# A two-layer hybrid decoder trunk on one core: the ring of expert weight buffers, the order of the shared product and the gather, and the first and last transfers

## The chip, the core and the metric

One core of one Trainium2 chip runs the whole program in one launch. The metric is the device time of that launch in microseconds (us), as the median of several runs; lower is better. TensorE is called PE below, VectorE DVE, ScalarE ACT, GpSimd POOL, and SyncE, which only issues transfers here, SP.

## What is computed

The reference runs two layers over 256 tokens of width 1024, all in float32. Each layer has three parts, each of them closed by a LayerNorm of alpha times its input plus its result:

```
mix = parallel_mixer(x, ...)            # short convolution branch and latent attention branch, gated
xat = memory_cross_attention(x, mem)    # k = mem @ w_xk, v = mem @ w_xv, 4 heads
ffn = moe_ffn(x, ...)                   # 64 experts of width 256, 8 per token, plus one shared expert

def experts(args):                      # every expert, weighted by its gate (zero where not chosen)
    hid = silu(einsum('btd,edf->btef', xt, w_gate)) * einsum('btd,edf->btef', xt, w_up)
    return einsum('btef,efd->btd', hid * gt[..., None], w_down)
shared = (silu(x @ ws_gate) * (x @ ws_up)) @ ws_down
```

The three weights of one expert are 1 MiB each, so the 64 experts of a layer are 192 MiB that must be read from HBM, and each is read once.

## The kernel before

Every engine has its own program, written out by hand, and they are ordered by semaphores. SP issues nearly all loads, in one fixed order; before a load into a buffer that was used earlier it waits (helper `alone`) until PE has read what lies there.

**Dense part of a layer.** 24 named loads (`LOADS`) of about 2 MiB go round six slots of the tile `ring`. PE multiplies them (`by_token`, `by_feature`, all through `accumulate`, L728) into the four PSUM banks `work0` to `work3`, which ACT and DVE copy out. The very first one is `xk0`, half of w_xk, which is multiplied with memT, the transposed memory; `mem` is loaded first of all, transposed by PE (L761) and copied by DVE (L1414).

**Routing.** DVE computes from the router scores which 8 experts each token takes, by a long chain of small instructions (L1701 to L1734), and signals `chosen_ready`. PE then computes the places of the tokens in each expert's list ("place", L1013, L1014). The shared expert's down product is eight matmuls into the PSUM banks `moe_sum0` to `moe_sum3` (`add_shared`, L1021), four behind "place" and four between the gathers. After the last one PE signals `shared_down`, which frees ring slot 5 (the load "down_router"). A gather (L1035) is four matmuls that select rows of x into a bank, which ACT (even chunks, L1361) or DVE (odd chunks, L1790) copies to SBUF; the first eight gathers of a layer alternate between banks 3 and 1.

**Experts.** They are taken in 32 pairs, eight pairs to a body, four bodies to a round (`expert_body`, L1099). There would be further rounds only if some expert had over 32 tokens of either half; in these runs there is one. A pair q of a body needs three units of 2 MiB: unit 3q and 3q+1 hold the gate and up weights, 3q+2 the two down weights. For a pair that is "not in halves" unit 3q is one expert and 3q+1 the other, and PE needs both to begin. For a pair "in halves" unit 3q holds the first half of the contraction for both experts and 3q+1 the second, so PE can begin with the first unit alone (`in_halves`). The order on PE in a pair is: gate and up (16 matmuls, L1128), half of the scatter of the pair before (L1082), a gather for a later batch (L1035), the transpose of the hidden rows (L1146), the other half of the scatter, the down product (8 matmuls, L1159), another gather. Below, units are numbered through a layer: unit m of body j is number 24j + m, and pairs are numbered 0 to 31.

**Buffers for the units.** Units 0 to 5 are the slots of `ring`; two more (6 and 7, tile `arena`) lie in memory that is free in the expert part; and one, `EXTRA`, lies in the first 4096 columns of `arena`. EXTRA is used once in a layer, for unit 8. `place_of` gives unit m of the first body its buffer, `wait_unit_read` gives the read that SP waits for before it loads:

```
if first:
    prev = m - UNITS - 1 if m <= 2 * UNITS else m - UNITS
elif second and m < UNITS:
    prev = m - (UNITS - 1) if m < UNITS - 1 else m - 2 * UNITS + 1
else:
    prev = m - UNITS
```

So a load waits for the read of the unit nine before it up to number 16, eight before it from 17 to 23, seven before it from 24 to 30 (31 finds its buffer free early), and eight before it from 32 on. The first nine units, numbers 0 to 8, are loaded in the dense part as their buffers come free; number 5 is the last of them to be issued, since it waits for `shared_down`. Number 9 waits for the read of number 0.

**The end.** After the second layer DVE normalises: token tile 0 is written by one instruction (L1506) and stored by SP (L599), tile 1 by two multiplies (L1511) and one add of 1024 columns (L1513), then stored whole (L601).

## Time and profile before

| | us |
|---|---|
| median of 3 runs | 1678.62 (1678.43 to 1679.38) |
| the profiled execution, its own time | 1679.52 |
| its span, first to last instruction | 1677.7 |
| PE busy in the span | 1618.2 (96%) |
| ACT busy, DVE busy, POOL busy | 280.5, 423.4, 80.5 |
| HBM read over the span | 507.64 MB, 303 GB/s mean |

The expert parts run from 380.7 to 838 us (first layer) and from 1204.8 to 1662 us (second layer); before each lies its dense part. PE is busy nearly everywhere, so what can be gained lies in the little idle time, and in what ended each stretch of it. A row of the profile's windows gives, for a stretch, each engine's busy time with its instruction count, the granted clock, the busy share of the 16 DMA engines and what they moved. A row of the waits names who waited for whom, total, number and longest. A row of the timeline has start, duration, engine, line, what it does, and in brackets the idle time before it with what ended it. [...]

### The profile page before, as it was taken

Reading aid. Unit: us, or ns where it says so; the run is one execution under the profiler, and the core shown is the slowest. Engines: PE = TensorE matmul, PEld = TensorE weight load, DVE = VectorE, ACT = ScalarE, POOL = GpSimd, SP = SyncE. Lnnn points to the kernel's source line nnn. Section 1 sums busy time; section 2 is a strip of 40 time slices with the busy share of each in tenths; the row PEclk is TensorE's granted clock in tenths of the full one; section 3 lists DMA queues with packets and bytes.
Section 4 is the critical chain, followed back from the end, with each engine's and each line's share of the span. In section 5 each row is a group of like instructions: output and inputs, shape, how many; then the busy total and the mean of one; then the engine's idle time right before and its main releaser. Section 6 shows DMA issues by size and latency. Waiting matters only on the chain.

```text
span 1677.7 us, 19829 instructions
## 1 busy us (share of the span) xinstructions
PE 1618.2 (96%) x8037; PEld 901.8 (54%) x8037; DVE 423.4 (25%) x886; ACT 280.5 (17%) x555; POOL 80.5 (5%) x92
## 2 busy tenths in 40 slices
PE   7999999999999999989999999999999999999996
PEld 5878867573333333333378786765633333333332
DVE  2122221162222222222222402112522222222223
ACT  1022011031111111111110410111311111111111
POOL 1000020030000000000030000201200000000000
PEclk9999999999999999999999999999999999999998
DMA  9246443469999999999980743434799999999995
GB/s 347 75 149 252 143 156 135 176 226 373 372 407 421 418 421 421 418 421 421 410 301 0 289 162 126 165 142 176 276 385 394 421 421 419 421 421 419 421 421 216
DMA packets 111240, 509.95 MB, mean 304 GB/s; under 512 B 8354, under 2 KB 12580, under 8 KB 68660
## 3 DMA queue, kind: packets, MB, share of 16 engines
q1 hardware_dynamic: 110592, 508.59, 76.2%
q8 instruction: 65, 1.06, 0.3%
q0 software_dynamic: 224, 0.12, 0.0%
q14 instruction: 19, 0.16, 0.0%
q10 hardware_dynamic: 340, 0.02, 0.0%
HBM read 507.64 MB, written 1.05 MB: 303 GB/s over the span
## 4 chain that ended last, share of the span: by engine, by line
PE 79%; DMA 12%; SPq 5%; DVE 3%; issue 1%; ACT 1%; DVEq 0%
PE work L728 38%; PE work L1128 20%; DMA ring<-in_w_up 11%; PE work L1159 9%; SPq L548 5%; PE moe_sum L1082 3%; PE work L1035 3%; PE moe_sum L1021 1%; DMA ring<-in_w_xk 1%; PE work L1146 1%; PE moe_sum L1074 1%; PE work L1042 0%; PE work L777 0%; PE work L864 0%; DVE arena L1721 0%
## 5 line engine op out<-in xcount | busy, mean ns | idle before, releaser
L1128 PE MATMUL work<-ring,arena 128*64 128x512 f32 x1536 | 365.5, 599 | 19.6 <-DMA ring<-in_w_up 12.4
L728 PE MATMUL work<-XT,ring 128*128 128x256 f32 (+1 forms) x1408 | 280.3, 360 | 1.3 <-DVE arena L1630 1.3
L728 PEld LDWEIGHTS work<-XT,ring 128*128 128x128 f32 x1408 | 247.5, 190 | 32.7 <-issue 3.0
L1128 PEld LDWEIGHTS work<-ring,arena 128*64 128x64 f32 x1536 | 118.4, 137 | 206.8 <-issue 194.7
L1159 PE MATMUL work<-ring,hidden 128*64 128x512 f32 x768 | 175.4, 598 | 1.0 <-DVE hidden L1829 1.0
L1836 DVE TENSOR_TENSOR out_lo<-work,out_hi 128x512 fp32r<-128x512 f32 x128 | 88.6, 692 | 231.1 <-ACT out_hi L1391 231.1
L1128 PE MATMUL work<-arena 128*64 128x512 f32 x512 | 136.6, 598 | 10.0 <-DMA ring<-in_w_up 7.4
L728 PE MATMUL work<-ring,arena 128*128 128x512 f32 (+1 forms) x336 | 140.4, 577 | 0.0
L1825 DVE SCALAR_TENSOR_TENSOR hidden<-hidden,slot_gate,work 128x256 f32<-128x256 f32 x64 | 30.8, 481 | 419.5 <-ACT hidden L1387 419.5
L1391 ACT CAST out_hi<-work 128x512 fp32r<-128x512 f32 x128 | 75.1, 587 | 213.6 <-PE work L1159 213.6
L1387 ACT ACTIVATE hidden<-work 128x256 f32<-128x256 f32 x64 | 24.6, 385 | 497.0 <-PE work L1128 497.0
L1159 PEld LDWEIGHTS work<-ring,hidden 128*64 128x64 f32 x768 | 50.9, 136 | 100.4 <-issue 84.1
L728 PEld LDWEIGHTS work<-ring,arena 128*128 128x128 f32 x336 | 63.7, 190 | 71.7 <-issue 65.1
L1128 PEld LDWEIGHTS work<-arena 128*64 128x64 f32 x512 | 42.4, 137 | 92.4 <-issue 84.5
L1035 PE MATMUL work<-sel,x_hi 128*128 128x256 f32 x288 | 91.9, 341 | 0.0
L1035 PEld LDWEIGHTS work<-sel,x_hi 128*128 128x128 f32 x288 | 54.0, 188 | 66.4 <-issue 64.8
L632 POOL TENSOR_TENSOR small<-small,minus_half 128x1 f32<-128x1 f32 x20 | 11.2, 559 | 1461.1 <-DVE small L1480 1459.4
L1035 PE MATMUL work<-sel,x_lo 128*128 128x256 f32 x288 | 75.8, 285 | 0.0
L1082 PE MATMUL moe_sum<-out_hi,selT 32*128 32x512 f32 x512 | 64.5, 494 | 1.8 <-DVE out_lo L1836 1.6
L728 PE MATMUL work<-memT,ring 128*128 128x256 f32 x256 | 58.9, 393 | 2.3 <-DMA ring<-in_w_xk 2.3
L1159 PE MATMUL work<-arena,hidden 128*64 128x512 f32 x256 | 58.5, 598 | 0.0
L1082 PEld LDWEIGHTS moe_sum<-out_hi,selT 32*128 32x128 f32 x512 | 24.5, 181 | 60.8 <-issue 52.3
(217 smaller groups left out, 1309.6 us busy)
## 6 DMA issues: line engine op xcount, KB each, us to landing
ring<-in_w_gate SPq DMA_DIRECT2D x96, 1024.0 KB, 19.2
ring<-in_w_up SPq DMA_DIRECT2D x96, 1024.0 KB, 21.2
ring<-in_w_down SPq DMA_DIRECT2D x96, 1024.0 KB, 19.0
arena<-in_w_down SPq DMA_DIRECT2D x32, 1024.0 KB, 18.1
arena<-in_w_gate SPq DMA_DIRECT2D x32, 1024.0 KB, 22.2
arena<-in_w_up SPq DMA_DIRECT2D x32, 1024.0 KB, 22.3
ring<-in_w_in SPq DMA_DIRECT2D x28, 1024.0 KB, 13.0
ring<-in_w_xk SPq DMA_DIRECT2D x8, 1024.0 KB, 9.0
```

The costliest lines, as they stand in the source:

```text
L548: sp.dma_start(dst, src).then_inc(slot_loaded[u], 16)
L728: mm = pe.matmul(dst, a, b, start=(k == 0), stop=(k == len(pairs) - 1))
L1021: return pe.matmul(moe_sum[2 * t + half][:, :], sharedT[:, c, t * P:(t + 1) * P], w_down_sb[:, c, half * BANK:(half + 1) * BANK], start=(c ...
L1035: mm = pe.matmul(dst[:, :, t, :], part[:, t, c * P:(c + 1) * P], src, start=(part is x_hi), stop=(part is x_lo))
L1074: pe.matmul(moe_sum[i][:, :].rearrange("p (q c) -> p q c", c=KC), ident_r[:, :], rows, start=False, stop=False, skip_group_check=True)
L1082: mm = pe.matmul(moe_sum[2 * (q % TT) + half][:, :], selT[rows, b, k, :], part[rows, half * BANK:(half + 1) * BANK], start=False, stop=Fal ...
L1128: mm = pe.matmul(work[0][rows, :], gathered_pair(b, c, k)[:, rows], w, start=(c == 0), stop=(c == KC - 1))
L1159: mm = pe.matmul(w[rows, :], hidT[:, c, rows], wd[:, e, c, half * BANK:(half + 1) * BANK], start=(c == 0), stop=(c == 1))
L1387: act.activation(hid, work[0][:, 0:EXPERT_DIM], ACT.Silu).then_inc(silu_ready, 1)
L1391: act.copy(out_hi[:, half * BANK:(half + 1) * BANK], work[1 + half][:, :]).then_inc(hi_ready[half], 1)
L1825: dve.scalar_tensor_tensor(out=hid, in0=hid, scalar=slot_gate[:, b, k:k + 1], in1=work[0][:, EXPERT_DIM:2 * EXPERT_DIM], op0=ALU.mult, op1 ...
L1836: dve.tensor_tensor(out_lo[:, cols], work[1 + half][:, :], out_hi[:, cols].bitcast(F32), ALU.subtract).then_inc(lo_ready[half], 1)
```

## The change

It has five parts.

1. **One ring of nine for three bodies.** EXTRA is gone. In bodies 0 to 2 unit number n goes to buffer n % 9, and each load waits for the read of the unit nine before it. From body 3 on there are eight buffers, and each load waits for the read of the unit eight before it.
2. **Halves.** Pairs 0 to 2 stay in halves. Before, the last pair of every body was too; now only pairs 28 to 31, the last four of the last body, are.
3. **Shared product and gather.** Two of the eight shared matmuls stand ahead of PE's wait for the routing and six right behind "place", so that `shared_down` comes ahead of the first gather and none is left between the gathers. The first eight gathers go round three banks (3, 1, 2), so each waits for the copy of the one three before. On DVE the product that makes the shared expert's activation of tile 0 moves ahead of the group ranking, and that of tile 1 to the place where tile 0's was.
4. **First loads.** `mem` is loaded as two tiles with a semaphore each; the first half of `xk0` has a semaphore of its own and PE begins with it, waiting for the second half only at chunk 4; the copies of memT are shared by ACT and DVE; the transpose of the small parameters moves behind the first half of `xk0`'s products; POOL issues its seven small parameter loads only after x has landed; DVE copies x before it works out the rotary angles.
5. **Last store.** The last add and the store of tile 1 are split in two halves of the columns.

The diff, cut to what matters:

```diff
-EXTRA = UNITS
+LONG = UNITS + 1
+LONG_BODIES = 3
+FIRST_BANKS = (3, 1, 2)
...
-        def in_halves(q, first=False):
-
-            return q == BODY_PAIRS - 1 or (first and q < 3)
-
-        def place_of(m, first=False):
-
-            if not first:
+        def in_halves(q, j):
+
+            return q < 3 if j == 0 else q >= BATCH if j is None else False
+
+        def place_of(m, j):
+
+            if j is None:
                 return m % UNITS, m // UNITS + 1
-            return (m, 1) if m <= UNITS else ((m - UNITS - 1) % UNITS, (m - UNITS - 1) // UNITS + 2)
+            n = j * 3 * BODY_PAIRS + m
+            return n % LONG, n // LONG + 1
...
-            def wait_unit_read(m, pairs, halves, first=False, second=False):
-
-                if first:
-                    prev = m - UNITS - 1 if m <= 2 * UNITS else m - UNITS
-                elif second and m < UNITS:
-                    prev = m - (UNITS - 1) if m < UNITS - 1 else m - 2 * UNITS + 1
-                else:
-                    prev = m - UNITS
-                q, part = divmod(prev, 3)
+            def wait_unit_read(m, pairs, halves, j=None):
+
+                q, part = divmod(m - (UNITS if j is None else LONG), 3)
                 if part == 2:
                     alone(sp, down_filled[1], snap(sp, pairs + (q + 1)))
...
+            sp.sem_inc(slot_loaded[0], 16)
+            for t in range(TT):
+                sp.dma_start(mem_sb[:, t, :], m2[t * P:(t + 1) * P, :]).then_inc(mem_loaded[t], 16)
...
+                        if l == 0 and n == 0 and i == 0:
+                            sp.dma_start(dst, src).then_inc(first_half_loaded, 16)
...
-                load_body(base, first, range(EXTRA + 1, UNITS * RING_USES), True)
-                load_body(base + 1, firsts(1), range(UNITS * RING_USES), second=True)
-                load_body(base + 2, firsts(2), range(UNITS * RING_USES))
+                for j in range(LONG_BODIES):
+                    load_body(base + j, firsts(j), range(0 if j else LONG, UNITS * RING_USES), j)
...
-                alone(sp, down_filled[1], snap(sp, (base + 1) * BODY_PAIRS + (EXTRA // 3 + 1)))
+                alone(sp, down_filled[1], snap(sp, (base + LONG_BODIES + 1) * BODY_PAIRS))
                 load_ln(l, ln3_g, ln3_b, 2)
...
+            pool.wait_ge(x_loaded, 16)
             for j, w in enumerate((ln1_g, ln1_b, ln2_g, ln2_b, ln3_g, ln3_b)):
...
+                def first_weights(k):
+                    if k % 2 == 0:
+                        pe.wait_ge(taken[k // 2], SETUP_USES)
+                    if k == KC // 2:
+                        wait_load(uses, "xk0")
...
+                for c in range(2):
+                    add_shared(0, 0, c)
                 pe.wait_ge(chosen_ready, l + 1)
...
-                shared_products = [(t, half, c) for t in range(TT) for half in range(2) for c in range(2)]
-                for t, half, c in shared_products[0:4]:
-                    add_shared(t, half, c)
+                for t, half in ((0, 1), (1, 0), (1, 1)):
+                    for c in range(2):
+                        mm = add_shared(t, half, c)
+                mm.then_inc(shared_down, 1)
...
                 for c in range(KC):
-                    if c >= 2:
-                        pe.wait_ge(gather_ready[c % 2], before * (KC // 2) + c // 2)
-                    gather(c, (3, 1)[c % 2])
-                    if c % 2 == 0:
-                        mm = add_shared(*shared_products[4 + c // 2])
-                        if c == KC - 2:
-                            mm.then_inc(shared_down, 1)
+                    if c >= 3:
+                        pe.wait_ge(gather_ready[(c - 3) % 2], before * (KC // 2) + ((c - 3) // 2 + 1))
+                    gather(c, FIRST_BANKS[c % 3])
...
                 then(dve.tensor_tensor(group_score, top2[:, :, 0], top2[:, :, 1], ALU.add))
+                share(0)
...
-                share(0)
+                share(1)
                 then(dve.tensor_tensor(weight, score, chosen, ALU.mult))
...
-                tell(dve.tensor_tensor(X[:, 1, :], X[:, 1, :], gb[:, 1, :], ALU.add), ln_applied, l * 3 + 4)
+                for half in range(2):
+                    cols = slice(half * BANK, (half + 1) * BANK)
+                    tell(dve.tensor_tensor(X[:, 1, cols], X[:, 1, cols], gb[:, 1, cols], ALU.add), layer_done, half + 2)
```

How it moves instructions shows at two places. The first is SP's order in the expert part of the first layer, where unit number 17 is loaded (the down weights of pair 5); `gate_up_done` and `down_filled_1` are the reads by gate-up and by down matmuls. Before:

```order
L548 DMA arena<-in_w_gate 128x2048 [waits gate_up_done]
L548 DMA arena<-in_w_up 128x2048
L548 DMA ring<-in_w_down 128x2048 [waits gate_up_done]
L548 DMA ring<-in_w_down 128x2048
L548 DMA ring<-in_w_gate 128x2048 [waits gate_up_done]
L548 DMA ring<-in_w_up 128x2048
L548 DMA ring<-in_w_gate 128x2048 [waits down_filled_1]
```

With the change:

```order
L552 DMA arena<-in_w_gate 128x2048 [waits gate_up_done]
L552 DMA arena<-in_w_up 128x2048
L552 DMA arena<-in_w_down 128x2048 [waits down_filled_1]
L552 DMA arena<-in_w_down 128x2048
L552 DMA ring<-in_w_gate 128x2048 [waits gate_up_done]
L552 DMA ring<-in_w_up 128x2048
L552 DMA ring<-in_w_gate 128x2048 [waits gate_up_done]
```

The down load went to the ninth buffer and waits for a down read (pair 2's) where it waited for a gate-up read (pair 3's). The two lines after it are unit 18, which waits as before for a gate-up read, now of unit 9 where it was of unit 10; both are read by the same matmuls.

The second place is PE between the last shared gate-up products and the first gathers. Before:

```order
L728 MATMUL work<-XT,ring 128x128 x40
L1013 MATMUL work<-arena,earlier 128x128
L1014 MATMUL work<-arena 128x128
L1021 MATMUL moe_sum<-ring,arena 128x512 x4
L1035 MATMUL work<-sel,x_hi 128x8x32
```

With the change:

```order
L734 MATMUL work<-XT,ring 128x128 x40
L1033 MATMUL moe_sum<-ring,arena 128x512 x2
L1042 MATMUL work<-arena,earlier 128x128
L1043 MATMUL work<-arena 128x128
L1033 MATMUL moe_sum<-ring,arena 128x512 x6
L1057 MATMUL work<-sel,x_hi 128x8x32
```

Two shared matmuls moved ahead of "place", where PE waits for the routing, and four came from between the gathers to ahead of them.

## Rows read from the trace of the kernel before

**Rows 1.** The page's first part: busy time of each engine.

```profile
PE 1618.2 (96%) x8037; PEld 901.8 (54%) x8037; DVE 423.4 (25%) x886; ACT 280.5 (17%) x555; POOL 80.5 (5%) x92
```

**Rows 2.** Waits of PE from 655 to 840 us: total, times, longest.

```profile
PE work L1128 <- DMA ring<-in_w_up: 11.5, 7, 2.7
PE work L1128 <- issue: 2.4, 2, 1.3
PE work L1128 <- DMA arena<-in_w_up: 1.2, 1, 1.2
```

**Rows 3.** Windows: PE, PEld, DVE, ACT, POOL busy, PEclk, DMA share, GB/s.

```profile
425.00:475.00 50.00, 50.00 (x272) 19.02 (x270) 10.76 (x19) 7.41 (x14) 0.00 (x0) 1.00 0.93 368
475.00:660.00 185.00, 183.31 (x1000) 71.12 (x998) 46.92 (x83) 31.37 (x58) 0.00 (x0) 1.00 1.01 421
660.00:831.00 171.00, 156.62 (x854) 63.47 (x852) 38.02 (x67) 25.34 (x47) 0.00 (x0) 1.00 1.01 419
1240.00:1300.00 60.00, 59.62 (x325) 23.35 (x326) 14.09 (x25) 9.75 (x18) 0.00 (x0) 1.00 0.94 376
1484.00:1655.00 171.00, 159.83 (x854) 63.97 (x856) 38.40 (x68) 25.32 (x47) 0.00 (x0) 0.98 1.01 418
```

**Rows 4.** Timeline of SP's queue: units 5, 9, 16 and 17 of the first layer.

```profile
380.33 0.81 SPq L548 DMA_DIRECT2D ring<-in_w_down  x2
384.41 0.33 SPq L548 DMA_DIRECT2D ring<-in_w_gate  x1
...
415.13 0.43 SPq L548 DMA_DIRECT2D arena<-in_w_up  x1
428.94 0.80 SPq L548 DMA_DIRECT2D ring<-in_w_down  x2
```

**Rows 5.** Timeline of PE: pair 30 of the first layer, then the start of pair 31.

```profile
810.78 7.09 PE L1128 MATMUL work<-ring,arena 128*64 128x512 f32 x32 [1.41 <-DMA ring<-in_w_up]
820.06 3.65 PE L1159 MATMUL work<-ring,hidden 128*64 128x512 f32 x16
...
824.98 3.65 PE L1128 MATMUL work<-ring,arena 128*64 128x512 f32 x16 [0.19 <-ACT hidden L1366]
```

**Rows 6.** DMA from issue to landing (min/median/max): expert units; xk0's two halves, first and second layer.

```profile
DMA to landing us min/median/max: 4.7/20.3/31.0
DMA to landing us min/median/max: 9.2/10.7/12.2
DMA to landing us min/median/max: 19.0/20.3/21.6
```

**Rows 7.** The chain that ended last: xk0's matmuls in the first and second layer.

```profile
13.98 16.86 PE work L728 x64
...
840.96 14.01 PE work L728 x64
```

**Rows 8.** Windows of the matmuls on memT alone: us, PE busy (records), PEclk, DMA share, GB/s.

```profile
15.00:16.00 1.00, 1.00 (x4) 1.00 1.01 389
21.00:22.00 1.00, 1.00 (x6) 1.00 1.09 394
```

**Rows 9.** Timeline of the routing's end and the first gathers, first layer.

```profile
368.81 0.42 DVE L1741 SCALAR_TENSOR_TENSOR arena<-arena,work 128x256 f32<-128x256 f32 x1
368.83 0.49 PE L1013 MATMUL work<-arena,earlier 128*128 128x128 f32 x2 [1.03 <-DVE arena L1734]
...
369.38 3.61 PE L1021 MATMUL moe_sum<-ring,arena 128*128 128x512 f32 x8
...
376.26 0.68 DVE L1786 TENSOR_REDUCE slot_gate<-hidden 128x4 f32<-128x512 f32 x1
...
380.65 7.09 PE L1128 MATMUL work<-ring,arena 128*64 128x512 f32 x32
```

**Rows 10.** Timeline of PE in the second layer: a gate-up under a lower clock.

```profile
1545.31 8.78 PE L1128 MATMUL work<-ring,arena 128*64 128x512 f32 x32 [2.17 <-DMA ring<-in_w_up]
```

**Rows 11.** Timeline of the end of the span, and the last store's landing.

```profile
1673.45 1.22 DVE L1513 TENSOR_TENSOR X<-X,arena 128x1024 f32<-128x1024 f32 x1
1674.70 0.34 SPq L601 DMA_DIRECT2D out<-X  x1
...
DMA to landing us min/median/max: 2.6/2.6/2.6
```

167 lines of the change are left out of this document (90 added, 77 removed).

## The prediction

> **What bounds the kernel now.** I read the page first, then PE's waits, then the windows of the DMA engines, then SP's queue. PE is busy for 1618.2 of 1677.7 us [rows 1], so at most some 60 us are idle, and the question is what ends each idle stretch. In the expert part of the first layer the waits answer it: from 655 us on PE waits 11.5 + 2.4 + 1.2 = 15.1 us for weights [rows 2]. The two waits put down to "issue" are such waits too, since they stand at the start of a gate-up like the others. The windows show why [rows 3]. From 475 us on the DMA engines are never idle, at 421 and then 419 GB/s. A unit is 2.097 MB, so it takes 5.0 us and a pair's three units 15.0 us, while PE does a pair in 13.5 us: the gate-up of pair 30 starts at 810.78, pair 31's at 824.98, 14.2 us later, of which 0.6 is the transposes of a batch that this pair alone has [rows 5]. So PE starts with nine units loaded or under way, eats 1.5 us of that lead in each pair, and has none left from about pair 20 on. Then the end of the layer is set by the bytes, that is by every microsecond in which the DMA engines stood still before. They stood still: from 425 to 475 us they moved 368 GB/s instead of 421, which is 53/421 x 50 = 6.3 us lost, and in the second layer from 1240 to 1300 us 45/421 x 60 = 6.4 us [rows 3]. PE was fully busy in both, so no wait of PE shows these holes.
>
> SP's queue shows what made them [rows 4]. Unit 16 is out at 415.1 us, unit 17 only at 428.9, when pair 3's gate-up had been read. One load in that place is a hole of its own, and seven buffers instead of eight for numbers 24 to 30 make the rest.
>
> **The ring of nine.** I follow the DMA engines unit by unit: each begins a unit when the last is through, or 2.2 us after its issue, whichever is later. The 2.2 is from the quickest half unit, 4.7 us from issue to landing, less 2.5 us for its 1.05 MB at 421 GB/s [rows 6]. PE's pairs start at 380.7 + 13.5 each (0.6 more once in four, 1.1 more in pairs 4 to 7 of a layer for the added input); a first-half unit is read 3.5 us into its pair, a whole gate or up 7.1 in, a down unit 12.9 in. For the kernel before this gives holes of 3.7 us before unit 17 and 2.8 before unit 25, 6.5 in all against 6.3 measured, so I trust it. With nine buffers unit 17 waits for the read of unit 8, at 420.5, while the engines are busy with unit 16 until 426.6: no hole. The tightest places left are unit 18, issued at 428.9, which must be under way when 17 ends at 431.6, so 0.5 us to spare, and unit 30 with 2.7. From number 72 on there are eight buffers again, but by then the engines are over 20 us behind the issue and it costs nothing. So 6.3 us of holes go.
>
> **Unit 5 earlier.** It is issued at 380.33, behind the last shared matmul, and so it is through at 380.3 + 2.2 + 5.0 = 387.5, and unit 9, issued at 384.41, at 392.5 [rows 4]. With the change all eight shared matmuls end before the gathers, at about 375.5 (below). Unit 5 is through at 383, and unit 9 at 384.4 + 2.2 + 5.0 = 391.6: 0.9 us gained. The other 4 us are not, since unit 9 waits for PE.
>
> **Halves at the end.** Pair 30 begins when its second unit is there, at 810.78 [rows 5]. In halves it begins one unit earlier, is through with 3.5 us of work when the second arrives, and ends gate-up 3.5 us after that instead of 7.1. Pair 31 is then 3.5 us earlier at its first half, and its second half, due 15.0 us after pair 30's second unit, holds it up for 1.0. Gain 2.5 us. Pairs 28 and 29 begin earlier too, but pair 30 waits for its units all the same. The last pairs of bodies 0 to 2 (7, 15 and 23) lose their halves, which costs nothing: by the same reckoning pair 25 is the first that waits for weights.
>
> **Routing and gathers.** PE is idle for 1.03 us before "place" [rows 9]. Two shared matmuls now fill that, at 3.61 / 4 = 0.90 us each, 1.8 us. They overrun the wait by 0.8. DVE's chain has the 0.42 us product ahead of the ranking, so the routing comes 0.4 to 0.5 later, which the two matmuls cover; behind it DVE has one product less and asks for "place" at the same time as before. PE is free for the gathers at 369.4 + 0.8 + 6 x 0.90 = 375.6. Before, the work from 372.8 to 380.65 held four shared matmuls (3.6 us) and 4.3 us of gathers and transposes. Alone they would end at 379.9. But the seventh gather needs the copy of the fourth, and DVE makes that after selT and the 0.68 us reduction [rows 9]; I work out 0.9 us of waiting. So pair 0 starts 0.15 us later than now. The bounds are 0.8 earlier (no wait) and 0.8 later (twice the wait).
>
> **Between the layers.** The second layer's xk0 lands at 817.2 + 21.6 = 838.8, PE uses it at 840.96 [rows 6, 7], a margin of 2.1 us. PE's end comes 6.3 + 0.9 + 2.5 - 0.15 = 9.55 us earlier, the landing only 7.05. So a new wait of 0.4 us.
>
> **Start.** The halves of xk0 land at 1.3 + 9.2 = 10.5 and 1.8 + 12.2 = 14.0 us [rows 6], and PE starts at 13.98. Now four matmuls can be done between. In the second layer the same 32 matmuls take 14.01 us, 0.44 each; here they take 16.86, since until about 19.7 us only four records pass in a microsecond and then six to seven [rows 7, 8]. That is the ratio of the two levels of the clock, 1.2 and 2.4 GHz, though the granted clock reads 1.00 in both rows. If the clock rises at the same moment, the four are worth 4 x 0.44 = 1.8 us; bounds 0 and 3.5 (four at the low level). I take 1.8.
>
> The Trainium skill, "TensorE: Matmul & The Clock Gate", part 1, says that the low level is the default and that activity releases it. By that, four matmuls and then a stall could let it rise earlier or later than now; by the first the start gives 3.5, by the second nothing. The later POOL loads and the second engine for the copies have no price of their own: PE waits for xk0 then, not for them.
>
> **End.** Half of the last add (0.6 of 1.22 us) runs beside the store of the other half, but the last store can start only where it starts now, at 1674.70; its 2.6 us are for 512 KB [rows 11], and at 256 KB they shrink by 0.6 at 421 GB/s, at least by nothing. I take 0.4.
>
> **Sum.** First layer 9.55 - 0.4 = 9.15, second 9.6, start 1.8, end 0.4: 20.95 us. The profiled execution took 1679.5, so 1658.6; the median of the runs is 0.9 lower, so **1657.7 us**. Adding up the bounds of the gathers, the start and the end gives 1653.5 to 1661.5, and half a microsecond on each DMA margin widens it a little.
>
> **Rivals.**
> *The holes stay.* If a load takes 3 us to get going, not 2.2, or PE reads a unit later than I reckon, unit 18's 0.5 us of margin is gone and holes come back behind it. What remains is the halves, unit 5, start and end: 2 x 3.3 + 2.2 = 8.8, or with half of the holes 15. Time 1663.5 to 1670. Against it: the same reckoning gave 6.5 for 6.3 before. Chance 0.12.
> *PE becomes the bound.* If the bytes come faster, all of PE's waits go: 15.1 in the first layer and 171.0 - 159.8 = 11.2 of idle time in the second [rows 2, 3], with start and end 28.5. Time 1650. For it nothing but two arena buffers more in use; 421 GB/s is the same from 475 us to 660 whatever is loaded. Chance 0.06.
> *Slower: TensorE's clock.* In the second layer one gate-up took 8.78 us instead of 7.09 in a stretch whose mean granted clock was 0.98 [rows 3, 10], so the chip at times grants the 1.2 GHz level though PE works. The waits that I remove are PE's rest. If it is granted less once these are gone, each such fall costs 1.7 us. Against a gain of 21 us it decides from 12 falls on, and 15 make the kernel slower: 1683. Against it: from 475 to 660 us PE was busy for 183.3 of 185 us with the clock at 1.00 [rows 3]. Chance 0.03.
> *The change does nothing there.* The order shows unit 17 on the ninth buffer with a down read as its wait, so the waits are what the text says. Chance 0.01, 1675.
>
> **Chances.** My forecast has 0.78. The range from 1651.0 to 1665.0 takes in its own spread and the nearer part of the first two rivals. 0.2% is 3.4 us, about what a measurement of this kernel can tell from no change. Faster by more 0.94, within 0.02, slower 0.04.
>
> **What would show it.** GB/s from 425 to 475 us at about 420. The lead of the transfers lasts to about pair 24 instead of 20, and PE's waits for expert weights come down from 15.1 us to about 6 in the first layer. Unit 17 is issued near 420.7. Pair 30's gate-up shows a wait in its middle. Pair 0 starts at 380.8 less what the start gains. Wrong would be: a stretch below 415 GB/s between 390 and 820 us, a wait of over 1.5 us in the gathers, or a start of the second layer's xk0 that is less than 8 us earlier beyond the start's gain.

## The result, and the profile after

| | before | after |
|---|---|---|
| median of 4 runs on one chip, us | 1679.0 (1678.43 to 1680.14) | 1656.85 (1656.42 to 1657.4) |
| ratio | | 0.9871, 95% interval 0.9858 to 0.9883 |
| the profiled execution, its own time | 1679.52 | 1656.67 |
| its span | 1677.7 | 1654.9 |

The change gains 22 us. 1657.7 was forecast, so the total is right within a microsecond. That closeness is luck: it is a sum of terms of which two were far too small and one too large, and they are taken apart here. In the code of after the gate-up stands in L1146, the down product in L1177, the gather in L1057, the shared product in L1033, "place" in L1042, xk0 in L734, the transposes of mem in L768 and of XT in L781, the expert loads in L552. A float32 matmul shows as two records in these views.

Windows of after, in the columns of [rows 3], at the same times in the first layer, where pair 0 starts 6.0 us earlier, and 20 us earlier in the second, where it starts 14.9 us earlier:

```profile
425.00:475.00 50.00, 50.00 (x264) 18.93 (x262) 12.76 (x22) 8.19 (x15) 0.00 (x0) 1.00 1.01 421
475.00:660.00 185.00, 184.44 (x1010) 71.02 (x1006) 44.49 (x79) 29.98 (x56) 0.00 (x0) 1.00 1.01 421
660.00:831.00 171.00, 163.02 (x901) 66.78 (x898) 43.79 (x81) 27.53 (x51) 0.93 (x2) 1.00 1.02 415
770.00:805.00 35.00, 32.70 (x186) 12.50 (x184) 7.27 (x13) 5.26 (x10) 0.00 (x0) 1.00 1.02 413
1220.00:1280.00 60.00, 59.62 (x320) 23.05 (x318) 13.66 (x24) 9.15 (x17) 0.00 (x0) 1.00 1.01 421
```

The holes are gone: 421 GB/s stand where [rows 3] has 368 and 376. But from 660 us on there are 415 where there were 419, and 413 from 770 to 805 us, where the loads in halves run. I had not expected that, and the prediction had named a stretch below 415 GB/s between 390 and 820 us as a sign of being wrong. PE is busy 6.4 us more from 660 to 831 us.

SP's queue in after, units 5, 9 and 17:

```profile
369.81 0.82 SPq L552 DMA_DIRECT2D ring<-in_w_down  x2
378.37 0.33 SPq L552 DMA_DIRECT2D ring<-in_w_gate  x1
...
414.53 0.80 SPq L552 DMA_DIRECT2D arena<-in_w_down  x2
```

Pair 0 starts at 374.61, so unit 17 is issued 39.9 us into the expert part; before it was 48.3 [rows 4, 9]. Unit 5 is issued 4.8 us ahead of pair 0, where it was 0.3.

PE's waits in after from 640 to 835 us, to be read against [rows 2]:

```profile
PE work L1146 <- DMA ring<-in_w_up: 4.2, 4, 1.4
PE work L1146 <- DMA arena<-in_w_up: 2.1, 2, 1.3
PE moe_sum L1100 <- DVE out_lo L1859: 0.8, 1, 0.8
PE work L734 <- DMA ring<-in_w_xk: 0.4, 1, 0.4
```

Of 15.1 us of waiting for weights 6.3 are left, and there is the new wait for xk0. The last wait of that kind in the first layer, on PE's timeline, with pair 30, the start of pair 31, and xk0 of the second layer:

```profile
793.32 3.65 PE L1146 MATMUL work<-ring,arena 128*64 128x512 f32 x16
798.42 3.65 PE L1146 MATMUL work<-ring,arena 128*64 128x512 f32 x16 [1.44 <-DMA ring<-in_w_up]
...
809.17 3.65 PE L1146 MATMUL work<-ring,arena 128*64 128x512 f32 x16 [0.19 <-ACT hidden L1388]
813.60 3.65 PE L1146 MATMUL work<-arena 128*64 128x512 f32 x16 [0.78 <-DMA arena<-in_w_up]
...
826.57 13.65 PE L734 MATMUL work<-memT,ring 128*128 128x256 f32 x62 [0.42 <-DMA ring<-in_w_xk]
```

Pair 30 waits in its middle and not at its start [rows 5]. The first wait for weights stands at 721.60, in pair 25.

The start, on PE's timeline:

```profile
5.24 3.84 PE L768 MATMUL work<-ident,arena 128*128 128x128 f32 x16 [5.24 <-DMA arena<-in_mem]
9.95 1.99 PE L734 MATMUL work<-memT,ring 128*128 128x256 f32 x8 [0.87 <-DMA ring<-in_w_xk]
12.74 5.42 PE L734 MATMUL work<-memT,ring 128*128 128x256 f32 x24 [0.80 <-DMA ring<-in_w_xk]
...
18.26 7.17 PE L734 MATMUL work<-memT,ring 128*128 128x256 f32 x32
25.27 1.94 PE L781 MATMUL work<-ident,arena 128*128 128x128 f32 x16
```

These are the 64 records of xk0, four matmuls (8 records) ahead of the second half. 32 records take 7.17 us at the 2.4 GHz level; the first 32 take 1.99 + 5.42 here, so they are at that level too. The trace's record of the granted clock says the same: it begins with the full level, at 9.08 us here and at 19.64 before. The windows print 1.00 for what lies ahead of that, which is why both of [rows 8] read 1.00. The transposes of XT begin at 25.27 where they began at 30.67 (timeline of before).

The routing's end in the first layer, to be read against [rows 9]:

```profile
362.24 1.88 PE L1033 MATMUL moe_sum<-ring,arena 128*128 128x512 f32 x4
363.96 0.38 PE L1042 MATMUL work<-arena,earlier 128*128 128x128 f32 x2
...
364.40 5.32 PE L1033 MATMUL moe_sum<-ring,arena 128*128 128x512 f32 x12
369.16 0.68 PE L1057 MATMUL work<-sel,x_hi 128*128 128x256 f32 x1
...
373.45 0.39 PE L1057 MATMUL work<-sel,x_hi 128*128 128x256 f32 x1 [0.40 <-DVE arena L1813]
...
374.61 7.09 PE L1146 MATMUL work<-ring,arena 128*64 128x512 f32 x32
```

PE's 1.03 us ahead of "place" are gone, and the only wait in the gathers is 0.40. The end:

```profile
1649.83 0.35 SPq L602 DMA_DIRECT2D out<-X  x1
1651.04 1.29 DVE L1536 TENSOR_TENSOR X<-X,arena 128x512 f32<-128x512 f32 x2
1651.75 0.93 SPq L606 DMA_DIRECT2D out<-X  x2
```

From five marks of PE in the two traces the 22.8 us of span are laid out like this (before, after, us):

| from | to | before | after | gain |
|---|---|---|---|---|
| start | transposes of XT | 30.67 | 25.27 | 5.40 |
| these | pair 0, layer 1 | 349.98 | 349.34 | 0.64 |
| pair 0 | xk0 of layer 2 | 460.24 | 451.96 | 8.28 |
| xk0 | pair 0, layer 2 | 363.88 | 363.26 | 0.62 |
| pair 0 | last scatter | 460.16 | 452.32 | 7.84 |
| last scatter | end of span | 12.77 | 12.75 | 0.02 |

For the expert part I took single units from the view of one line's DMA issues, which gives the time from issue to landing. Unit 9, whose two transfers SP issues at 384.4 and 384.8 us before and at 378.4 and 378.7 after, before and then after:

```profile
DMA to landing us min/median/max: 6.7/7.8/8.8
```

```profile
DMA to landing us min/median/max: 4.7/5.8/6.8
```

The issue stands 3.8 us after pair 0's start in both, so the unit is there 12.9 us after it before (384.79 + 8.8 - 380.65) and 10.9 after (378.75 + 6.8 - 374.61). Read in the same way, by the later of a unit's two transfers, in us after pair 0's start, first layer:

| unit | 5 | 9 | 17 | 24 | 30 | 83 | 91 | 94 | 95 |
|---|---|---|---|---|---|---|---|---|---|
| before | 6.8 | 12.9 | 55.5 | 94.2 | 124.5 | 390.2 | 430.0 | 445.2 | 450.2 |
| after | 4.0 | 10.9 | 52.0 | 86.8 | 116.7 | 381.9 | 423.8 | 439.0 | 443.9 |
| gain | 2.8 | 2.0 | 3.5 | 7.4 | 7.8 | 8.3 | 6.2 | 6.2 | 6.3 |

So 2.0 us are there at unit 9, and the holes give 5.8 more by unit 30. Up to unit 83, the last before the units in halves, it stays; from there to unit 91 two microseconds are lost again, and that loss stays to the last unit, which is a whole one. Single landings scatter by up to 1 us.

### The profile page after: what moved, and what is told of

It reads as the page before. It is cut to its first block, busy times and chain, and to the rows that moved or that the text cites. A ratio compares the mean times of both kernels' runs of the same rounds, so it can differ in the third digit from the quotient of the medians.

```text
span 1654.9 us, 19841 instructions
## 1 busy us (share of the span) xinstructions
PE 1612.9 (97%) x8037; PEld 895.9 (54%) x8037; DVE 421.7 (25%) x885; ACT 282.6 (17%) x558; POOL 80.4 (5%) x92
## 2 busy tenths in 40 slices
DMA packets 111400, 509.95 MB, mean 308 GB/s; under 512 B 8386, under 2 KB 12612, under 8 KB 68820
## 4 chain that ended last, share of the span: by engine, by line
PE 83%; SPq 8%; DMA 6%; DVE 1%; issue 1%; ACT 1%; DVEq 0%
PE work L734 40%; PE work L1146 21%; PE work L1177 10%; SPq L552 7%; PE moe_sum L1100 4%; PE work L1057 4%; DMA arena<-in_w_up 3%; DMA ring<-in_w_xk 2%; DMA ring<-in_w_up 2%; PE moe_sum L1033 1%; PE work L1164 1%; PE moe_sum L1092 1%; PE work L1064 0%; PE work L781 0%; PE work L883 0%
## 5 line engine op out<-in xcount | busy, mean ns | idle before, releaser
L1146 PE MATMUL work<-ring,arena 128*64 128x512 f32 x1408 | 312.7, 595 | 10.1 <-DMA ring<-in_w_up 8.2
L734 PE MATMUL work<-XT,ring 128*128 128x256 f32 (+1 forms) x1408 | 280.3, 360 | 1.3 <-DVE arena L1653 1.3
L734 PEld LDWEIGHTS work<-XT,ring 128*128 128x128 f32 x1408 | 247.5, 190 | 32.7 <-issue 3.0
L1146 PEld LDWEIGHTS work<-ring,arena 128*64 128x64 f32 x1408 | 99.4, 137 | 195.0 <-issue 176.2
L1177 PE MATMUL work<-ring,hidden 128*64 128x512 f32 x704 | 160.8, 598 | 1.0 <-DVE hidden L1852 1.0
L1146 PE MATMUL work<-arena 128*64 128x512 f32 x640 | 142.2, 595 | 5.9 <-DMA arena<-in_w_up 4.7
L734 PE MATMUL work<-ring,arena 128*128 128x512 f32 (+1 forms) x336 | 140.4, 577 | 0.0
L734 PEld LDWEIGHTS work<-ring,arena 128*128 128x128 f32 x336 | 63.7, 190 | 71.7 <-issue 65.0
L1177 PEld LDWEIGHTS work<-ring,hidden 128*64 128x64 f32 x704 | 46.6, 136 | 92.1 <-issue 76.1
L1146 PEld LDWEIGHTS work<-arena 128*64 128x64 f32 x640 | 45.7, 137 | 91.2 <-issue 84.6
L1057 PE MATMUL work<-sel,x_hi 128*128 128x256 f32 x288 | 89.3, 333 | 0.8 <-DVE arena L1813 0.8
L1057 PEld LDWEIGHTS work<-sel,x_hi 128*128 128x128 f32 x288 | 54.1, 188 | 64.9 <-issue 63.7
L1057 PE MATMUL work<-sel,x_lo 128*128 128x256 f32 x288 | 75.6, 286 | 0.0
L1177 PE MATMUL work<-arena,hidden 128*64 128x512 f32 x320 | 73.1, 598 | 0.0
L734 PE MATMUL work<-memT,ring 128*128 128x256 f32 x256 | 56.6, 381 | 2.1 <-DMA ring<-in_w_xk 2.1
## 6 DMA issues: line engine op xcount, KB each, us to landing
arena<-in_w_down SPq DMA_DIRECT2D x40, 1024.0 KB, 18.5
```

The lines of the kernel that those rows point to most:

```text
L734: mm = pe.matmul(dst, a, b, start=(k == 0), stop=(k == len(pairs) - 1))
L1057: mm = pe.matmul(dst[:, :, t, :], part[:, t, c * P:(c + 1) * P], src, start=(part is x_hi), stop=(part is x_lo))
L1146: mm = pe.matmul(work[0][rows, :], gathered_pair(b, c, k)[:, rows], w, start=(c == 0), stop=(c == KC - 1))
L1177: mm = pe.matmul(w[rows, :], hidT[:, c, rows], wd[:, e, c, half * BANK:(half + 1) * BANK], start=(c == 0), stop=(c == 1))
```

## The experiments

The question was which term is worth what: the ring of nine, unit 5, the halves, the start. Each variant undoes or alters one part of the changed kernel. They ran on three chips, on which the kernel before took 1679.49, 1678.98 and 1678.81 us (1679.0 beside the change), so half a microsecond between variants of different chips says nothing. The mean granted clock of an execution is 0.997 where it has no fall in the midst of its work, and 0.001 less for each short fall; in all eight executions of the change it is 0.997.

**The lead of nine.** The ring of nine keeps its buffers and the first loads their wait, but from unit 17 on each load waits for the read of the unit eight before it, in all bodies:

```diff
-                q, part = divmod(m - (UNITS if j is None else LONG), 3)
+                q, part = divmod(m - (LONG if j == 0 and m <= 2 * UNITS else UNITS), 3)
```

> The change with its nine buffers, but from unit 17 on each load waits for the read of the unit eight before it, as with eight buffers. Theory (idle DMA engines early set the end): one hole of 4.7 us before unit 17 comes back in each layer, the stretch from 419 to 469 us falls from 421 to about 380 GB/s, PE's waits for weights rise from 6.3 to about 11 us a layer, and the time is 9.4 us longer than the change: about 1666. Rival (the lead did not matter, the gain came from start, gathers and halves): within 1 us of the change, 1657.

Measured: 1666.73 us (1666.26 to 1667.19), ratio 0.9923 (0.9907 to 0.994), 9.9 more than the change. SP's queue, windows and PE's waits (640 to 835 us) of this variant:

```profile
422.88 0.80 SPq L552 DMA_DIRECT2D arena<-in_w_down  x2
```

```profile
415.00:420.00 5.00, 4.81 (x25) 1.78 (x25) 2.22 (x4) 0.64 (x2) 0.00 (x0) 1.00 0.96 395
420.00:425.00 5.00, 5.00 (x38) 2.16 (x34) 0.90 (x2) 0.97 (x2) 0.00 (x0) 1.00 0.22 54
425.00:430.00 5.00, 5.00 (x28) 1.92 (x26) 1.40 (x3) 1.17 (x2) 0.00 (x0) 1.00 1.01 426
```

```profile
PE work L1146 <- DMA ring<-in_w_up: 7.0, 6, 1.4
PE work L1146 <- DMA arena<-in_w_up: 3.0, 3, 1.3
PE work L734 <- DMA ring<-in_w_xk: 2.0, 1, 2.0
```

The second layer's xk0, in the chain that ended last:

```profile
831.73 15.77 PE work L734 x64
```

Unit 17 is issued 8.4 us later and the DMA engines all but stand still for five microseconds (54 GB/s). PE is fully busy in those same five (5.00 of 5.00), and pays between 640 and 835 us, where it waits for 12.0 us in place of 6.7. That is the theory of the prediction, reproduced: a hole in the loads at 420 us is a wait of PE at 800. By the marks the expert parts are 5.2 and 3.7 us longer than in the change (457.13 and 456.04), for a hole reckoned at 4.7. The rest is the clock: right behind the wait of 2.0 us for xk0 it falls to the 1.2 GHz level, and xk0 takes 15.77 us where it took 14.08, 1.7 more. The mean granted clock of all four executions is 0.996 or 0.995, so the median has such a fall in it too.

**The gather and shared order.** "place", the eight shared matmuls, the banks and DVE's products are put back as they were; ring, halves, start and end stay:

```diff
                 for c in range(KC):
-                    if c >= 3:
-                        pe.wait_ge(gather_ready[(c - 3) % 2], before * (KC // 2) + ((c - 3) // 2 + 1))
-                    gather(c, FIRST_BANKS[c % 3])
+                    if c >= 2:
+                        pe.wait_ge(gather_ready[c % 2], before * (KC // 2) + c // 2)
+                    gather(c, (3, 1)[c % 2])
+                    if c % 2 == 0:
+                        mm = add_shared(*shared_products[4 + c // 2])
...
```

> The change with the shared product, the first gathers' banks and DVE's two products as before. Theory: PE's wait before place comes back (0.6 us a layer in the two traces), and unit 5 goes out behind the gathers again, so that unit 9 lands about 1 us later against pair 0's start: together 1.6 us a layer, about 1660. The prediction gave this part a loss of 0.15 and a gain of 0.9 a layer: 1658.5. Rival: unit 5 does not matter since the engines idle before unit 9 anyway: 0.6 a layer, 1658.

Measured: 1663.27 us (1663.19 to 1663.54), ratio 0.9904 (0.9888 to 0.9921): 6.4 more, more than either theory gave. SP's queue, and xk0 of the second layer in the chain that ended last:

```profile
376.22 0.82 SPq L552 DMA_DIRECT2D ring<-in_w_down  x2
380.30 0.33 SPq L552 DMA_DIRECT2D ring<-in_w_gate  x1
```

```profile
830.46 15.77 PE work L734 x64
```

Pair 0 starts at 376.54, unit 5 is issued 0.3 us ahead of it as before the change, and unit 9 lands 13.4 us after it (10.9 in the change). Some 2 us of this stay to the end of the layer: unit 30 lands at 118.6 where the change has 116.7, unit 95 at 445.9 where it has 443.9, and xk0 starts 453.92 us after pair 0 where it has 451.96. So unit 5's place is worth 2 us in the first layer, not the 0.9 I forecast. Of the rest, 0.6 a layer is the routing and gathers themselves, 1.3 us come from the start (TensorE's lower level lasted to about 14.9 us in this execution), and 1.7 from a fall of the clock in xk0 (15.77 us where the change has 14.08). Neither of these two can be laid on the edit. In the second layer only 0.4 to 0.8 us of longer expert part remain. So of the 6.6 us of this execution some 3.6 go by the edit (2.0 and 0.4 in the expert parts, 0.6 twice), near the 3.2 of the theory, and 3.0 by the start and the fall. The mean granted clock of all four executions is 0.995 or 0.996, so falls are in the median as well.

**How the start stands.** The first loads, copies and POOL's issues are put back:

```diff
-            for t in range(TT):
-                sp.dma_start(mem_sb[:, t, :], m2[t * P:(t + 1) * P, :]).then_inc(mem_loaded[t], 16)
+            sp.dma_start(mem_sb, m2.rearrange("(t p) d -> p t d", p=P)).then_inc(mem_loaded[0], 16)
...
-            pool.wait_ge(x_loaded, 16)
...
                     pe.wait_ge(first_half_loaded, 16)
+                    wait_load(uses, "xk0")
...
```

> The change with the whole start as before: mem in one load, PE waiting for all of xk0, all copies of memT on DVE, POOL's small loads at once, x copied late. The two traces put 5.4 us on the start, where the prediction had 1.8: expected 1662.2 and a rise of the clock at about 20 us again (matmuls on memT four records a microsecond until then). If the rise of the clock in the two traces was chance, it can be at 9 us here too and the time is 1659.3.

Measured: 1663.57 us (1661.02 to 1664.2), ratio 0.9907 (0.989 to 0.9923): 6.7 more. xk0's 64 records stand at 15.03 and take 16.10 us, and the transposes of XT begin at 30.97. This is the fastest of the four executions, with a mean granted clock of 0.997; the other three have 0.994, that is falls of the clock elsewhere, and they make the median. So it is the marks that price the start: the transposes are 5.0 and 5.7 us later than in two profiles of the change. The nine profiles in which the changed start stands unaltered have them at 24.98 to 26.58, so the start is worth 4 to 6 us, not 1.8. Three more kernels take it apart. PE waits for both halves of xk0:

```diff
                     pe.wait_ge(first_half_loaded, 16)
+                    wait_load(uses, "xk0")
```

> PE waits for both halves of xk0 before its first matmul, all else as in the change. If the start's gain comes from the clock (PE works from 9.95 us on and the full rate is there from 10 us, where before it was there from 19.7 us), PE now starts at 12.7 us and the 32 matmuls take more than 14.0 us: 14.0 plus half of whatever time is spent at the low rate, up to 17 us, so the transposes of XT begin at 27 to 30 us instead of 25.3: 1659 to 1661 us. If the gain comes only from the earlier landing of xk0 and the eight matmuls done early, the rate is full from the start, the transposes begin at 12.7 + 14.0 = 26.7 us, and the time is 1658.3.

Measured: 1660.89 us (1659.46 to 1661.91), ratio 0.9896 (0.9879 to 0.9913). Its timeline of PE:

```profile
12.54 8.83 PE L734 MATMUL work<-memT,ring 128*128 128x256 f32 x32 [3.60 <-DMA ring<-in_w_xk]
...
21.48 7.17 PE L734 MATMUL work<-memT,ring 128*128 128x256 f32 x32
28.49 1.94 PE L781 MATMUL work<-ident,arena 128*128 128x128 f32 x16
```

The first 32 records take 8.83 us, 1.7 over the 7.17 of the next 32, so the lower level of the clock is back for some 3.3 us. Here the windows show it (PE alone; the granted clock is the third number from the end):

```profile
12.00:13.00 1.00, 0.46 (x2) 0.89 0.99 397
13.00:14.00 1.00, 1.00 (x4) 0.50 1.02 406
```

The full level had been granted at 9.36 us, just behind the transposes of mem, and was taken back at 12.78, behind the 3.6 us in which PE was idle. To see whether PE's idle time ahead of them matters, the same kernel with work in that gap (the results of the 16 transposes are read by nobody):

```diff
+                    for _ in range(KEEP):
+                        pe.transpose(moe_sum[1][:, 0:P], ident[:, :], ident[:, :])
                     pe.wait_ge(first_half_loaded, 16)
+                    wait_load(uses, "xk0")
```

> As wait_for_whole_xk0, but PE does 16 transposes of the identity, which nobody reads, in the 3.6 us that it waits for xk0 there. xk0's matmuls start at 12.5 us in both. If it is PE's own earlier work that brings the full clock, the 64 records of xk0, 16.0 us there, take 14.0 to 14.5 us here and the transposes of XT begin at 26.6 to 27.0 us instead of 28.5: 1659.2 us. If the clock rises at its own moment (about 16 us there), nothing changes but noise: 28.5 us and 1660.9.

Measured: 1658.95 us (1658.58 to 1659.82), ratio 0.9883 (0.9866 to 0.9899), and on its timeline of PE:

```profile
8.86 1.91 PE L831 MATMUL moe_sum<-ident 128*128 128x128 f32 x16
12.74 7.14 PE L735 MATMUL work<-memT,ring 128*128 128x256 f32 x32 [1.96 <-issue]
...
27.00 1.95 PE L782 MATMUL work<-ident,arena 128*128 128x128 f32 x16
```

xk0 starts 0.2 us later and is through 1.5 us earlier, all of it at the 2.4 GHz level, and the median falls by 1.9 us (the ranges overlap in 1659.46 to 1659.82). The row of the added transposes says more: 16 of them take 1.91 us, as those of XT do (1.95), while the 16 of mem ahead of them took 3.48. So the full level was there when they began (the trace has it from 8.73 us), and they didn't bring it; with them in the gap, it was not taken back. One pair of profiles and four runs each, on two chips, is what this rests on, and in another execution the level may rise late in either kernel. The third kernel lets POOL issue its seven loads at once:

```diff
-            pool.wait_ge(x_loaded, 16)
```

> POOL no longer waits for the mem tile before it issues its loads; all else as in the change. If these loads compete with xk0 at the start, xk0's halves land later (10.5 and 13.9 us as before the change, instead of 9.9 and 12.6) and the transposes of XT begin up to 1.3 us later: 1657 to 1658.2 us. If the waiting is without effect: 1656.8.

Measured: 1659.69 us (1658.36 to 1660.36), ratio 0.9887 (0.987 to 0.9903), 2.9 more than the change. Its PE timeline:

```profile
10.68 9.12 PE L733 MATMUL work<-memT,ring 128*128 128x256 f32 x32 [1.60 <-DMA ring<-in_w_xk]
...
26.91 1.95 PE L780 MATMUL work<-ident,arena 128*128 128x128 f32 x16
```

xk0's first half is there 0.7 us later than in the change, and the 32 records run partly at the lower level again. The transposes of XT are 1.6 us late in this profile against the first of the change. But of two variants with an unaltered start, whose clock rises about as late as here (14.8 us for 14.5), both have them at 26.58, so the edit itself may be worth only 0.3 to 0.8 us. This is the fastest of the four executions; the others are 1 to 2 us slower still, two of them with a mean granted clock of 0.996, and what they lost isn't in a profile. I had priced POOL's wait at nothing; it is a part of the gain, and how large a part stays open.

**Halves.** Only the last pair of the last body in halves; none of them; and every unit of gate and up weights of every pair:

```diff
-            return q < 3 if j == 0 else q >= BATCH if j is None else False
+            return q < 3 if j == 0 else q == BODY_PAIRS - 1 if j is None else False
```

> The change with halves at the end for pair 31 alone (as before), not for pairs 28 to 31. By the prediction's term (2.5 us a layer for pair 30 begun one unit earlier, at the same rate of bytes) the kernel is 5 us slower than the change: about 1662. Rival: a gate or up unit loaded in halves takes longer than a whole one (about 5.15 us against 4.99, by the windows of the change, 413 to 415 GB/s from 745 us on against 421 before), which takes back about half of what the halves bring: 1.4 us a layer, about 1659.5, with 421 GB/s up to 800 us.

Measured: 1658.54 us (1658.18 to 1658.67), ratio 0.9876 (0.9859 to 0.9892): 1.7 more, 0.85 a layer, where the term of the prediction was 2.5 a layer. By the marks the expert parts are 1.3 and 0.5 us longer (453.26 and 452.84), with a short fall of the clock in each layer, right behind a wait of 2.5 us for weights (mean granted clock 0.94 from 770 to 800 us):

```profile
770.00:800.00 30.00, 27.48 (x144) 10.56 (x142) 6.37 (x11) 4.29 (x8) 0.00 (x0) 0.94 1.01 419
```

Unit 91 lands 422.8 us after pair 0 in this kernel and 94 at 438.0, in the change 423.8 and 439.0: in halves both come 1.0 us later.

```diff
+            return j == 0 and q < 3
```

> The last body's gate/up units are loaded whole; the first pairs of body 0 keep their halves. By the prediction (halves are worth 2.5 us a layer) 1662 us. By slower halves (each halved unit costs 0.1 to 0.15 us more, and six units of pairs 28 to 31 are in halves) the halves bring 2.5 less some 0.9, so 1.6 a layer: 1660 us. With one pair in halves the time was already 1658.5, so a value close to that would say that the last pair's halves bring next to nothing.

Measured: 1661.31 us (1660.42 to 1662.2), ratio 0.9895 (0.9878 to 0.9911): 4.5 more, 2.2 a layer. So the last pair in halves, as the kernel before had it too, is worth 1.4, and the three that the change adds 0.85.

```diff
+            return True
```

> Every gate/up unit of every pair is loaded in halves of 4 KB rows instead of whole; nothing else differs. Theory (halves load slower: 413 to 415 GB/s where the whole units have 421, so 5.09 to 5.15 us for a unit instead of 5.0): two thirds of the loads are gate/up units, and the end of each layer is set by the bytes, so about 8 us a layer are added (64 units less the 13 that the change has in halves already, x 0.10 to 0.15 = 5 to 8), 1667 to 1673 us in all, and the stretch from 475 to 660 us reads about 416 GB/s. Rival (the lower rate at the end belongs to the end of the layer, to xk0's loads among them, not to the halves): 421 GB/s from 475 to 660 us and 1657 us.

Measured: 1675.31 us (1672.04 to 1678.94, 10 runs), ratio 0.9977 (0.9967 to 0.9986), 18.5 more than the change run beside it (change_again). Its windows:

```profile
425.00:475.00 50.00, 50.00 (x266) 18.89 (x268) 13.13 (x23) 8.48 (x16) 0.00 (x0) 1.00 1.02 413
475.00:660.00 185.00, 184.44 (x1006) 70.94 (x1002) 44.50 (x78) 29.61 (x55) 0.00 (x0) 1.00 1.02 413
```

413 GB/s, not 421, with the DMA engines busy throughout (1.02). A unit of 2.097 MB takes 5.08 us on the mean where it took 4.98, and two of three units are gate and up units, so 0.15 us more for one in halves. The bytes are the same; the page of the profile counts 120020 packets under 8 KB instead of 68820, since a half has rows of 4 KB in HBM and a whole unit rows of 8 KB. That the smaller rows are the cause is likely and not shown by itself. The rival, that the lower rate belongs to the layer's end, is out. In the profiled execution 8.2 us are added between pair 0 and xk0 in the first layer (460.20 for 451.96) and 7.2 up to the last scatter in the second. Of the 8.2, 2.7 are there by unit 17: unit 9, the first in halves to be loaded behind pair 0's start, lands 14.0 us after it where the change has 10.9. That step the reckoning of 0.15 a unit had left out. The median is 2.7 us above this execution, the spread of the ten is wide, and what makes it isn't known.

Since six units more in halves cost 6 x 0.15 = 0.9 us a layer, one may ask for fewer:

```diff
-            return q < 3 if j == 0 else q >= BATCH if j is None else False
+            return q < 3 if j == 0 else q >= BATCH + 1 if j is None else False
```

> Halves for the last three pairs of each layer instead of the last four. By the unit-by-unit reckoning with 5.0 us for a whole unit and 5.1 for one in halves, pair 28's halves bring nothing that pair 29 does not wait for again, and two slower units are saved: 0.2 to 0.4 us a layer, 1656.2 us in all; a difference too small for the intervals, so the trace decides: the start of the second layer's xk0 against pair 0's start should be 451.6 us (452.0 in the change).

Measured: 1656.42 us (1655.14 to 1657.75), ratio 0.9863 (0.9847 to 0.988). xk0 stands 451.60 us after pair 0, as forecast to the hundredth, against 451.96 and 451.91 in two profiles of the change. In the second layer it is 452.45 against 452.32 and 451.89, so no gain there. In the runs it can't be told from the change.

**The end.** The last add and store undivided:

```diff
-            for half in range(2):
-                cols = slice(half * BANK, (half + 1) * BANK)
-                sp.wait_ge(layer_done, half + 2)
-                sp.dma_start(out_tiles[:, 1, cols], X[:, 1, cols]).then_inc(out_stored, 16)
+            sp.wait_ge(layer_done, 2)
+            sp.dma_start(out_tiles[:, 1, :], X[:, 1, :]).then_inc(out_stored, 16)
...
```

> The last add and the last store undivided, as before. By the prediction 0.4 us are lost: 1657.2 us, with 11.7 us from the first instruction of the last batch norm to the end of the span instead of 11.3. If the split brings nothing: 1656.8 and 11.3.

Measured: 1657.49 us (1657.24 to 1657.73), ratio 0.9873 (0.9856 to 0.9889). From the first instruction of the last batch norm (1643.72) to the end of the span (1655.5) it is 11.8 us, in the change 1654.9 - 1643.60 = 11.3: 0.5 us, close to the 0.4 forecast. In the totals, 0.6 to 0.7, it is too small to be sure of.

**The change once more.**

> The changed kernel itself once more, so that the variants of this job have it beside them on the same chip. Expected 1656.9 us. If the clock of TensorE falls at other places than in its first profile (which shows no fall), a gate-up of 8.8 instead of 7.1 us or an xk0 of 15.8 instead of 14.0 us will stand somewhere, each with 1.7 us, and the time may then be 1658.5.

Measured: 1656.77 us (1656.41 to 1658.44), ratio 0.9872 (0.9855 to 0.9888). No fall in the profile, but the start is another one:

```profile
9.89 9.02 PE L734 MATMUL work<-memT,ring 128*128 128x256 f32 x32 [0.95 <-DMA ring<-in_w_xk]
...
26.02 1.95 PE L781 MATMUL work<-ident,arena 128*128 128x128 f32 x16
```

The same kernel has the lower level until about 13.6 us here (9.02 - 7.17 = 1.85 us lost at half rate, so 3.7 us of it), and needs no stop for xk0's second half, since it is there by the time the slower matmuls ask for it. That costs 0.75 us against the first profile. Together with single falls of 1.7 us at other places this is what blurs differences of 1 to 2 us between kernels.

## Why the prediction was right

**What bounds the kernel: right.** The bytes set the end of each expert part, and a hole in the loads costs its full length some 400 us later. The holes were worth 6.3 us by forecast; between units 9 and 30 the loads gained 5.8. Unit 18's margin of 0.5 us held, since the windows show 421 GB/s up to 660 us. "The holes stay" and "PE becomes the bound" are both out, the latter since 6.3 us of waits are left. The eight-unit lead shows the mechanism in reverse.

**Unit 5 earlier: right in kind, half the size.** 0.9 a layer forecast, 2.0 measured at unit 9, and 2 in the first layer when the order was put back; in the second 1.4 at unit 9, and 0.4 to 0.8 when it was put back. The step that failed is the landing of unit 9 in the kernel before. After the change it lands 10.9 us after pair 0's start, where I had 10.8. Before it landed at 12.9, where I had 392.5 - 380.65 = 11.9: behind unit 5, which was through at 387.5 as reckoned, it came 6.1 us after that unit and not 5.0. The distance varies: 5.2 in the second layer, 6.4 and 6.0 with the order put back. The check against the 6.3 us of holes could not show this, since it concerns units 17 and 25 alone.

**Halves at the end: the term that was too large.** 2.5 a layer forecast, 0.85 by the run with one pair in halves. The mechanism is as described: gate-up of pair 30 ends 9.76 us earlier after pair 0's start (427.46 for 437.22) although unit 91 lands only 6.2 us earlier, so 3.5 us come from the halves, and pair 31's second half gives 1.0 back, as I had. The step that failed is the silent one that a unit in halves takes 5.0 us like a whole one. It takes 0.15 more, and by unit 91 and 94 they are 1.0 us late against the kernel with one pair in halves. That is also the 413 GB/s from 770 to 805 us, the sign of being wrong that did appear. It leaves 1.5 of the 2.5; the other 0.6 I can't lay on one thing.

**Between the layers: right.** 0.4 us of new waiting for xk0 forecast, 0.42 measured.

**Routing and gathers: wrong sign, small.** -0.15 forecast, +0.64 and +0.62 measured, inside the bound of 0.8. I worked out 0.9 us of waiting for the copy of the fourth gather; it was 0.40. The other 0.3 is shared matmuls ending earlier than my sum of idle, overrun and six durations.

**Start: far too small.** 1.8 forecast with bounds 0 and 3.5, 5.4 measured in the first profile and 4.65 in the second, outside both. The step that failed is "if the clock rises at the same moment", 19.7 us; it rose at 9.1 in the one and 13.7 in the other, and between 8.0 and 14.8 in all nine profiles that have this start. Of the 5.4 us, 1.8 are the four matmuls done ahead (4 x 0.44, the term that was forecast), 1.2 are the landing of xk0's second half (12.74 in place of 13.98), and the remaining 2.4 are the lower level gone: it cost 2.85 us before (16.86 - 14.01), less some 0.4 for the small transpose and the stop that now stand in the middle. The landing is the second thing I had left out: POOL's seven loads and the split load of mem had "no price of their own", and POOL's alone put xk0's first half off by 0.7 us.

The Trainium skill, "TensorE: Matmul & The Clock Gate", part 1, says that activity of the array releases the full clock, and that the point at which it does so varies between runs of one kernel. The traces agree on both: PE works from 5.2 us on, and the full level comes at 9.1 and 13.7 us in two profiles of the change. Of the two readings of that rule that the prediction held open the one with an early rise was the right one, and it was worth more than its 3.5 us, since the early landing came on top.

**End: right, and given back.** 0.4 forecast, 0.5 by the variant. But the last batch norm starts 1.45 us after the last scatter where it was 1.08; the variant with the undivided store has 1.43, so it is not the split's doing. What makes it isn't settled.

**The clock rival: the other way round.** Neither profile of the change shows a fall in the midst of its work; four of the eleven variants' profiles show one or two, and the kernel before has two. Behind the start they go with long waits of PE: six of the seven begin within some 1 us of the end of a wait for weights of 2.0 to 2.8 us, like that of [rows 10], and all the profiles together have only nine such waits. No wait for weights of the change behind the start is over 1.45 us. So the idle time that the change removes did nothing to keep the clock up; the long waits are where it fell. That goes by where they stand in these profiles, and no variant tested it by itself. The seventh, in gather_order_back, came behind two waits of 0.8 and 0.5 us. In a stretch bound by bytes a fall need not cost its 1.7 us: the second layer's expert part of the kernel before has two falls and takes 460.16 us, the first layer's has none and takes 460.24.

The sum came out near because errors of both signs met. By the table of marks: start +3.6, routing and gathers +0.8 and +0.8, the expert parts -1.0 (8.28 for 9.7 - 0.4) and -1.9 (7.84 for 9.7), the end -0.4, together +1.9. The second layer's 7.84 is 8.27 in the second profile of the change (451.89 us from pair 0 to the last scatter), so about half a microsecond of it is the run's.

## What to carry to other kernels

Where bytes bound a stage, look for the stretch in which the DMA engines stood still, even if PE was busy all through it: a hole closed by one buffer more comes back in full hundreds of microseconds later, and of a load issued 4.5 us earlier up to 2 us came back. Loading a tile in two halves lets the last consumers start sooner, but here rows of 4 KB instead of 8 KB cost 3% of the rate of such a unit, so at the end of the layer it belongs in the last three or four pairs and not before them (the first three pairs, which have it too, were not tried without). At the start of a program price the order of the first loads on all queues and the clock together: small loads on another queue, and an idle gap of a few microseconds on PE, can each cost about as much as the 1.8 us of matmuls that one sets out to hide.

## What the runs showed of the hardware

- 421 GB/s with 8 KB rows against 413 with 4 KB rows, over 235 us at a stretch, with the DMA engines busy in both (two of three units in halves in the second; that the row size is the cause is likely, not shown by itself).
- A unit of 2 MiB that found the queue nearly empty had landed 7.2 us after its first issue (unit 9 after the change); issued while another was under way, it landed 5.2 to 6.4 us after that one (unit 9 in both layers before and with the order put back).
- The full clock at the start came at 9.1 us in one profile and 13.7 in another of the same kernel, and from 8.0 to 14.8 in nine profiles with the same start. With PE idle for 3.6 us ahead of xk0 it was taken back, and 32 records took 8.83 us; with 16 short transposes in the gap it stayed, and they took 7.14.
- Of nine waits of PE for weights of 2.0 to 2.8 us behind the start six had the clock at its 1.2 GHz level within some 1 us of their end. One fall in all the profiles came without such a wait.
- POOL's seven small loads, issued while the first weights are on their way, put off the first half of xk0 by 0.7 us. The median was 2.9 us higher with them, in part by the clock.
